# Weaving the first scores of three attentions, and the index scores of the third, into the projections before them

## The chip, the cores and the metric

One core of a Trainium2 chip runs the whole program in one launch. The metric is device time in microseconds (us). Engines are named as in the profile: PE is TensorE, PEld its weight loads, DVE is VectorE, ACT is ScalarE, SP issues the weight DMAs.

## What is computed

The reference is a stack of four layers on one sequence of 256 tokens and 1024 features, all in float32. The part that matters here is the three attentions with 16 heads of 64 features, each after a projection that makes queries, keys and values:

```python
# 1 (chunked): k, v from one product, q from another; a bias per head
sc = einsum('bqhd,bkhd->bhqk', qb, kb) + bias;  p = softmax(sc);  o = p @ v;  o @ w_o
# 2 (even): 8 "forgetting" heads with a cumulated gate, 8 window heads with a sink and rotations
o = concatenate([o_fox, o_swa], -1) @ w_out
# 3 (odd): index scores choose the 64 keys that each query sees
logits = einsum('bqhd,bsd->bqhs', iqi, ik)
score = einsum('bqh,bqhs->bqs', iwi, relu(logits));  _, idx = top_k(score, 64)
s = q . k[idx];  o = softmax(s) @ v[idx];  o @ w_out
```

Feed-forward layers follow each attention, the last one a mixture of eight experts.

## The kernel before

**Weights as a stream.** Every product takes its weights from one stream of slots of 1 MB (128 x 2048 floats). SP loads slots into six buffers `raw` (L358). For each slot ACT copies it, rounded, to `whi` (`split`, L1055), and DVE makes the remainder `wlo = raw - whi` (L1527); both have three buffers (SPL). PE then multiplies a slot in `product` with three passes each (L437, L438, L439): 24 products 512 wide in all, first 12 for the first 128 tokens, then 12 for the second 128. A projection 512 wide takes two slots. `mid(j)` is called between the two halves of slot j, `after(j)` behind it. The stream order, `Plan`, also has modulation slots (`ada`): DVE reduces one with the conditioning vector (`modulate`, L1548 and L1550, four passes); after every second, PE turns the sum into a column (`ada_turn`, L646) and DVE takes it (`ada_cols`, L1572).

**Order by hand.** There is no planner: each engine's program is an in-order list, and semaphores join them. On ACT and DVE `used` counts the slots consumed and `split(n)` prepares slots up to n; `take` and `take_scaled` on ACT empty a finished product from PSUM (L1109, L1121) and raise `acc_free`.

**Before an attention.** Queries and keys are turned on PE in rounds of up to four 128 x 128 transposes (`rounds`, L529) into PSUM banks 6 and 7, and ACT copies each out (`copies`, L1092). In the first attention the last two rounds of keys' source and all four of the queries stand behind the last slot or near it; in the second, eight rounds of `fq` and `fk` stand around and behind the last slot.

**An attention** (`attention` in each engine) goes over eight pairs of heads. For pair p: PE `scores(p)` (L680); DVE `mask(p)`, adding a mask and taking the minimum (L1856); ACT `exps`, one call for each head, with the sum (L1245), and for window heads also the sink's exponential (L1249); DVE `weigh(p)` (L1866, L1869); PE `turn(p)`, six transposes into banks 6 and 7 (L691); DVE and ACT each copy one half out (L1877, L1257); PE `values(p)` (L703). After each second pair ACT and DVE split the output into `xhi` and `xlo` (L1261, L1882). Then the output projection's product begins. DVE has the first two of its slots, and the modulation behind the second, ready before `mask(0)`.

**The third attention** first has its own work. Its projection has five parts (slots 2, 1, 2, 2, 2): index queries; index key and weights; queries in two parts; keys and values. DVE rotates them (`rope`, L1906 to L1911, six operations for each 128 tokens). After the fourth part PE makes 16 index products (L846), ACT a relu of each (L1379), DVE adds each to `score` (L2059, L2061). DVE then finds the 64 largest in eight rounds (L2078, L2080), and makes the mask `dsab` (L2086 to L2096). `mask(0)` needs it. Fourth and fifth part are on either side of the index products.

**After an attention** comes its residual: DVE adds both halves of the output to `h`, in the second and third attention with a gate (L1635, L1636); in the second, `residual_normed` goes on to squares, root, normalisation (L1698) and transposes (L546) before the next product can start.

Of the kernel before, what the change touches and what calls it, by code (L numbers as in the profile page):

```python
# [26 lines left out]
P = 128  # L27
# [71 lines left out]
class Plan:  # L99
# [3 lines left out]
    def __init__(self):  # L103
# [38 lines left out]
        proj("q", D, layer=0, behind=odd)  # L142
# [4 lines left out]
        proj("e_in", E_IN, E_ORDER, layer=1, behind=odd[1:])  # L147
# [43 lines left out]
def build_program(nc, x_in, cols_in, rows_in, vg_in, fg1_in, fg_in, pos_in, ws_in, toep_in, rw_in, stream_in, out):  # L191
# [3 lines left out]
    with ctx:  # L195
# [69 lines left out]
        SM_C, PT_C = (sm_0, sm_1, two_of(tok[:, 0:768])), (two_of(tok[:, 1024:1792]), two_of(tok[:, 2048:2816]))  # L265
        SM_E, PT_E = (sm_0, sm_1, two_of(tok[:, 0:768])), (two_of(tok[:, 5376:6144]), two_of(tok[:, E_W:E_W + 768]))
# [19 lines left out]
        rt_o = [af[:, 1280 + n * 288:1280 + (n + 1) * 288] for n in range(4)]  # L286
        score = af[:, 2432:2944].rearrange("p (t k) -> p t k", t=NT)
        left = af[:, 2944:3456].rearrange("p (t k) -> p t k", t=NT)
        relu = af[:, 3456:3968].rearrange("p (b k) -> p b k", b=2)
# [27 lines left out]
        def head(q, k, v, mask, h):  # L317
# [6 lines left out]
        EVEN = ([head(fqT[:, hh], fkT[:, hh], te[:, :, E_FV + hh * DH:E_FV + (hh + 1) * DH],  # L324
                      lambda t: causal[:, S - (t + 1) * P:S], hh) for hh in range(8)]
                + [head(half(sqT, hh, hh // 2), half(skT, hh, hh // 4), te[:, :, E_SV + hh // 4 * DH:E_SV + (hh // 4 + 1) * DH],
                        lambda t: window[:, S - (t + 1) * P:S], 8 + hh) for hh in range(8)])
# [103 lines left out]
        def _(pe):  # L431
# [218 lines left out]
            def gate_blocks(layer, g, hf):  # L650

                def after(j):
                    if j == 1 or (layer == 1 and (g, hf) == (0, 1)):
# [10 lines left out]
            def attention(units, name, sm, pT, after=None, mid=None):  # L664
# [5 lines left out]
                cols_made = turned_before(name)  # L670
                if cols_made:
                    pe.wait_ge(sem("ada_taken"), cols_made)

                def scores(p):
                    if p >= 2:
                        pe.wait_ge(sem("att_m"), 2 * (b + p - 1))
                    for t in range(NT):
                        for e in range(2):
                            a = units[2 * p + e]
                            m = pe.matmul(ps[:, (4 if p % 2 else 2 * sc) + e, parts(t)], a["q"][:, t * P:(t + 1) * P],  # L680
                                          a["k"][:, 0:(t + 1) * P], start=True, stop=True)
                    m.then_inc(sem("att_s"), 1)
# [1704 lines left out]
```

## Time and profile before

| | us |
|---|---|
| three runs | 1570.97, 1572.42, 1575.75; median 1572.42 |
| the profiled execution | 1572.48 |
| its span in the trace | 1570.7 |
| DVE / ACT / PE busy | 1240.2 / 915.9 / 1471.8 |
| stretch from a projection's last product to the output projection's first: first, second, third attention | 34.49, 34.44, 44.68 |

The span is what the trace holds; 1.8 us lie around it. Engine times are sums of their instructions; matmuls are pipelined, and each is shown with its own end, so that they overlap a little.

### The profile page before, as it was taken

How to read it: one execution, taken by the hardware profiler on the slowest of the kernel's cores; microseconds unless marked ns; L12 is line 12 of the kernel's file. 1: busy time of each engine (PE TensorE's matmuls, PEld its weight loads, DVE VectorE, ACT ScalarE, POOL GpSimd, SP SyncE). 2: the span in 40 equal slices, each digit the busy share in tenths (PEclk: the TensorE clock that was granted, in tenths of full speed). 3: DMA queues.
4: the chain of work that ended last, by engine and by line, in shares of the span. 5: the costliest groups of instructions: out<-in, count | busy, mean ns of one | idle time of the engine just before them, and what ended most of it. 6: DMA issues, size and time to landing. Idle time of an engine off the chain costs nothing.

```text
span 1570.7 us, 19868 instructions
## 1 busy us (share of the span) xinstructions
PE 1471.8 (94%) x7238; PEld 1200.2 (76%) x7239; DVE 1240.2 (79%) x1722; ACT 915.9 (58%) x1202; POOL 5.1 (0%) x17
## 2 busy tenths in 40 slices
PE   7999999997999998988899998959999999999995
PEld 5888888885788887866788887747778878877883
DVE  6767889768667888777777886795888888898887
ACT  6656564547556654465433333554776787777674
POOL 0000000000000000000000000000000000000000
PEclk9999999999999999999999998979999999999997
DMA  9654448873345467643567784312588889888882
GB/s 350 235 222 154 173 168 302 318 270 134 134 164 192 167 227 269 241 161 111 186 254 267 252 320 172 108 54 81 200 323 306 312 302 338 307 312 325 303 315 92
DMA packets 53416, 358.16 MB, mean 228 GB/s; under 512 B 6096, under 2 KB 7120, under 8 KB 12640
## 3 DMA queue, kind: packets, MB, share of 16 engines
q1 hardware_dynamic: 52736, 354.77, 60.9%
q0 software_dynamic: 176, 2.13, 0.4%
q8 instruction: 45, 0.74, 0.2%
q10 hardware_dynamic: 432, 0.30, 0.1%
q14 instruction: 27, 0.22, 0.0%
HBM read 356.13 MB, written 1.05 MB: 227 GB/s over the span
## 4 chain that ended last, share of the span: by engine, by line
PE 68%; DVE 17%; ACT 7%; issue 6%; DMA 1%; PEldq 0%; DVEq 0%; PEld 0%; ACTq 0%; SPq 0%
PE ps L437 21%; PE ps L439 20%; PE ps L438 20%; DVE wlo L1527 6%; ACT whi L1055 3%; PE ps L916 2%; PE ps L595 1%; DVE tok L2224 1%; PE ps L646 1%; PE ps L529 1%; DVE attn_scratch L1856 1%; DMA raw<-stream_dram 1%; DVE tok L1775 1%; ACT attn_scratch L1245 1%; DVE tok L1709 1%
## 5 line engine op out<-in xcount | busy, mean ns | idle before, releaser
L1527 DVE TENSOR_TENSOR wlo<-raw,whi 128x2048 fp32r<-128x2048 f32 (+2 forms) x304 | 651.3, 2165 | 144.1 <-ACT whi L1055 131.0
L1055 ACT ACTIVATE whi<-raw 128x2048 fp32r<-128x2048 f32 (+2 forms) x304 | 547.5, 1819 | 233.2 <-PE ps L439 228.3
L437 PE MATMUL ps<-whi,xhi 128*128 128x512 f32 (+3 forms) x1360 | 536.5, 394 | 19.5 <-DVE wlo L1527 9.4
L439 PE MATMUL ps<-whi,xlo 128*128 128x512 f32 (+3 forms) x1360 | 524.0, 385 | 0.0
L438 PE MATMUL ps<-wlo,xhi 128*128 128x512 f32 (+3 forms) x1360 | 523.8, 385 | 0.0
L437 PEld LDWEIGHTS ps<-whi,xhi 128*128 128x128 f32 x1360 | 258.2, 190 | 81.0 <-DVE wlo L1527 13.0
L439 PEld LDWEIGHTS ps<-whi,xlo 128*128 128x128 f32 x1360 | 257.9, 190 | 52.3
L438 PEld LDWEIGHTS ps<-wlo,xhi 128*128 128x128 f32 x1360 | 258.5, 190 | 47.0
L437 PE MATMUL ps<-whi,ahi 128*128 128x512 f32 x440 | 177.9, 404 | 5.2 <-DVE wlo L1527 5.1
L439 PE MATMUL ps<-whi,alo 128*128 128x512 f32 x440 | 174.1, 396 | 0.0
L438 PE MATMUL ps<-wlo,ahi 128*128 128x512 f32 x440 | 173.2, 394 | 0.0
L1550 DVE SCALAR_TENSOR_TENSOR acc<-raw,cs,acc 128x512 f32<-128x512 f32 x168 | 126.2, 751 | 5.1
L437 PEld LDWEIGHTS ps<-whi,ahi 128*128 128x128 f32 x440 | 82.6, 188 | 28.8 <-DVE wlo L1527 8.9
L1775 DVE SCALAR_TENSOR_TENSOR tok<-ps,cols,tok 128x255 f32<-128x255 f32 (+1 forms) x176 | 72.7, 476 | 37.0 <-ACT tok L1205 36.2
L439 PEld LDWEIGHTS ps<-whi,alo 128*128 128x128 f32 x440 | 82.6, 188 | 20.3
L438 PEld LDWEIGHTS ps<-wlo,ahi 128*128 128x128 f32 x440 | 82.7, 188 | 18.4
L1109 ACT ACTIVATE tok<-ps,st 128x512 f32<-128x512 f32 x64 | 40.6, 686 | 45.8 <-PE ps L595 30.7
L1210 ACT ACTIVATE tok<-tok 128x512 f32<-128x512 f32 x22 | 14.0, 634 | 65.6 <-DVE tok L1775 65.6
L1205 ACT ACTIVATE tok<-ps,cols 128x256 f32<-128x256 f32 x88 | 42.7, 576 | 3.8 <-DVEq L1793 3.8
L1245 ACT ACTIVATE attn_scratch<-attn_scratch,sx 128x128 f32<-128x128 f32 x72 | 32.0, 445 | 19.8 <-DVE sx L1856 19.8
L680 PE MATMUL ps<-head_scratch 64*128 64x128 f32 (+3 forms) x192 | 29.1, 419 | 11.8 <-DVE sx L1856 9.5
L1439 ACT ACTIVATE tok<-ps 128x256 f32<-128x256 f32 (+1 forms) x48 | 17.7, 368 | 35.1 <-PE ps L439 35.0
(286 smaller groups left out, 1179.9 us busy)
## 6 DMA issues: line engine op xcount, KB each, us to landing
raw<-stream_dram SPq DMA_DIRECT2D x317, 1024.0 KB, 5.1
raw<-stream_dram SPq DMA_DIRECT2D x32, 512.0 KB, 4.3
attn_scratch<-toep_dram POOLq DMA_DIRECT2D x1, 2048.0 KB, 9.5
raw<-stream_dram SPq DMA_DIRECT2D x2, 528.0 KB, 4.4
h<-x_dram SPq DMA_DIRECT2D x2, 512.0 KB, 4.8
y<-tok SPq DMA_DIRECT2D x2, 512.0 KB, 2.7
head_scratch<-w_s_dram SPq DMA_DIRECT2D x1, 512.0 KB, 14.2
head_scratch<-vg_dram SPq DMA_DIRECT2D x1, 512.0 KB, 11.2
```

Source lines behind the costliest of these rows:

```text
L437: pe.matmul(o, xh, wh, start=start, stop=False)
L438: pe.matmul(o, xh, wl, start=False, stop=False)
L439: return pe.matmul(o, xl, wh, start=False, stop=stop)
L680: m = pe.matmul(ps[:, (4 if p % 2 else 2 * sc) + e, parts(t)], a["q"][:, t * P:(t + 1) * P], a["k"][:, 0:(t + 1) * P], start=True, stop=True)
L916: m = pe.matmul(ps[:, 5 + 2 * b, k * P:(k + 1) * P], TA[:, t, (4 * b + k) * P:(4 * b + k + 1) * P], G[:, t, :], start=t == 0, stop=t == NT ...
L1055: act.activation(whi[:, q % SPL, 0:w], raw[:, s % RAW, 0:w], ACT.Copy).then_inc(sem("hi_done"), 1)
L1109: m = act.activation(dst[:, t], src[:, t], func, scale=st[:, 6 + t:7 + t])
L1205: m = act.activation(conv[:, f, :], ps[:, 6 + f // 2, (f % 2) * S:(f % 2 + 1) * S], ACT.Identity, scale=sc, bias=bi)
L1245: m = act.activation(x, x, ACT.Exp, bias=neg_max(u, t), scale=-1.0, accum_out=total(u, t))
L1527: dve.tensor_tensor(wlo[:, q % SPL, 0:w], raw[:, s % RAW, 0:w], whi[:, q % SPL, 0:w].bitcast(F32), ALU.subtract).then_inc(sem("lo_done"), 1)
L1550: m = dve.scalar_tensor_tensor(acc[:, :], wk, cs[:, kk:kk + 1], acc[:, :], ALU.mult, ALU.add)
L1775: m = dve.scalar_tensor_tensor(o, src, cols[:, c:c + 1], o, ALU.mult, ALU.add)
```

## The change

- **Pieces between slots.** `scores` of pairs 0 and 1 become a function `first_scores`, called between the two last slots of the projection (first and second attention), or before the attention (third). The transposes that they need are moved ahead of them; the last rounds (queries 2 and 3, or the fox keys) run inside the attention, just before `turn(0)` (`between`). On ACT `exps` of the first four heads come before the last part is taken.
- **Splits.** Only the first slot of the output projection is prepared ahead of the attention. DVE prepares the second at the attention's end, `hold` puts off the modulation behind it until the last `lo`.
- **Modulation slots** behind the last slot of the projection go one slot earlier (`Plan`).
- **Second attention:** window heads come first; the rows of its output weights are rolled to match. Third score buffers go to other places.
- **Third attention:** four batches of four index products stand in the halves and between slots of parts three and four; four relu buffers in place of two; rotations for both halves of tokens at once, four operations in place of twelve; selection rounds around the last slots; the mask's last two steps made in one.

```diff
-        proj("q", D, layer=0, behind=odd)
+        proj("q", D, layer=0, behind=(1, 2))
-        proj("e_in", E_IN, E_ORDER, layer=1, behind=odd[1:])
+        proj("e_in", E_IN, E_ORDER, layer=1, behind=(3, 5, 7, 8))
...
+            def first_scores(units, name):
+                pe.wait_ge(sem("acc_free"), T("acc"))
+                scores(units, 0)
+                cols_made = turned_before(name)
+                if cols_made:
+                    pe.wait_ge(sem("ada_taken"), cols_made)
+                scores(units, 1)
...
-                scores(0)
-                for i in range(n + 2):
+                for i in range(1, n + 2):
                     if i + 1 < n:
-                        scores(i + 1)
+                        scores(units, i + 1)
+                    if i == 2:
+                        between()
...
+            def first_queries(j):
+                if j == 0:
+                    pe.wait_ge(sem("acc_free"), T("acc"))
+                    two(TA, 0)
+                    two(TA, 1)
+            def first_chunked(j):
+                if j == 0:
+                    pe.wait_ge(sem("tr_free"), T("tr", 1))
+                    first_scores(CHUNKED, "attn_out")
+                    pe.wait_ge(sem("tr_free"), T("tr"))
+            proj(W, mid=first_queries, after=first_chunked)
...
+            proj(width[2], mid=lambda j: index_scores(0) if j == 1 else None, after=index_turns)
+            proj(width[3], mid=lambda j: None if j else index_scores(2), after=gate_turns)
+            proj(width[4], after=gate_blocks(1, 1, 1, 0))
...
+            keys(3)
+            split(used[0] + 3)
+            queries(0)
+            queries(1)
+            for u in range(4):
+                exps(CHUNKED, u)
+            take_scaled(TA[:, :, W:D], ahead=1)
+            queries(2)
+            queries(3)
             attention(CHUNKED, PT_C)
...
+            split(used[0] + 3)
             copies([skT], first=2)
-            split(used[0] + AHEAD + 1)
             copies([fqT[:, 2 * r:2 * r + 2, :] for r in range(4)], scale=DH ** -0.5, first=3)
-            take(te[:, :, E_FV:E_FG])
+            for u in range(4):
+                exps(EVEN, u)
+            take(te[:, :, E_FV:E_FG], ahead=1)
...
+                split(used[0] + 2, hold=True)
+                lo(3)
                 split(used[0] + SPL)
-                lo(3)
...
+            def rotate(first, heads):
+                dve.tensor_tensor(xc, x, table(cosT), ALU.mult)
+                link(dve.tensor_tensor(xs, x, table(sinT), ALU.mult))
+                dve.tensor_tensor(part(x, 0), part(xc, 0), part(xs, 1), ALU.subtract)
+                link(dve.tensor_tensor(part(x, 1), part(xc, 1), part(xs, 0), ALU.add))
...
+            split(used[0] + 3)
+            add_index(0)
+            split(used[0] + 4)
+            add_index(1)
+            used[0] += 2
+            next_pair()
+            add_index(2)
+            split(used[0] + 3)
+            add_index(3)
+            both(lambda t, nk: dve.tensor_tensor(score[:, t, 0:nk], score[:, t, 0:nk], causal[:, S - nk:S], ALU.add))
+            link(dve.tensor_scalar(causal[:, :], causal[:, :], NEG, None, ALU.add))
+            used[0] += 2
+            next_pair()
+            split(used[0] + 2)
+            dve.wait_ge(sem("acc_free"), T.up("acc"))
+            rotate(0, 8)
+            largest(0)
+            dve.wait_ge(sem("acc_free"), T.up("acc"))
+            rotate(W, 8)
+            dve.sem_inc(sem("rope_done"), 1)
+            for n in range(1, 5):
+                largest(n)
+            used[0] += 2
+            next_pair()
+            split(used[0] + 1)
+            dve.wait_ge(sem("acc_free"), T.up("acc"))
+            rotate(2 * W, 4)
+            dve.sem_inc(sem("rope_done"), 1)
+            for n in range(5, TOPK // 8):
+                largest(n)
...
-            both(lambda t, nk: dve.tensor_scalar(gt[:, t, 0:nk], gt[:, t, 0:nk], -NEG, NEG, ALU.mult, ALU.add))
-            both(lambda t, nk: dve.tensor_tensor(dsab[:, t, 0:nk], gt[:, t, 0:nk], causal[:, S - nk:S], ALU.min))
+            both(lambda t, nk: dve.scalar_tensor_tensor(dsab[:, t, 0:nk], gt[:, t, 0:nk], -NEG, causal[:, S - nk:S],
+                                                        ALU.mult, ALU.add))
```

## Rows read from the trace of the kernel before

**Rows 1.** The page: the chain that ended last, shares of the span by engine

```profile
PE 68%; DVE 17%; ACT 7%; issue 6%; DMA 1%; PEldq 0%; DVEq 0%; PEld 0%; ACTq 0%; SPq 0%
```

**Rows 2.** Windows (us, busy of PE, PEld, DVE, ACT, POOL, clock, DMA share, GB/s)

```profile
362.65:397.14 34.49, 25.03 (x197) 17.42 (x196) 28.71 (x105) 26.76 (x85) 0.00 (x0) 0.90 0.25 98
687.65:722.09 34.44, 26.73 (x192) 18.89 (x191) 28.17 (x108) 27.28 (x98) 0.00 (x0) 0.90 0.15 59
1022.48:1067.16 44.68, 26.69 (x192) 18.57 (x190) 42.11 (x156) 26.59 (x86) 0.00 (x0) 0.77 0.13 47
1002.98:1011.29 8.31, 6.88 (x36) 5.25 (x34) 5.02 (x13) 5.94 (x16) 0.00 (x0) 0.79 0.34 127
```

**Rows 3.** Timeline of PE, first attention (start us, us, engine, line, operation)

```profile
356.92 0.48 PE L437 MATMUL ps<-whi,xhi 128*128 128x512 f32 x1
...
375.91 0.94 PE L691 MATMUL ps<-ident,attn_scratch 128*128 128x128 f32 x6
```

**Rows 4.** Timeline of DVE, first attention

```profile
371.79 0.29 DVE L1856 CUSTOM_DVE_ANT_0 attn_scratch<-ps,attn_scratch 128x128 f32<-128x128 f32 x1 [0.27 <-PE ps L680]
...
379.58 1.03 DVE L1869 TENSOR_TENSOR tok<-tok,sx 128x256 f32<-128x256 f32 x2
```

**Rows 5.** Timeline of ACT, first attention

```profile
364.46 1.91 ACT L1055 ACTIVATE whi<-raw 128x2048 fp32r<-128x2048 f32 x1
366.26 1.26 ACT L1109 ACTIVATE tok<-ps,st 128x512 f32<-128x512 f32 x2
368.82 1.09 ACT L1092 ACTIVATE head_scratch<-ps 128x512 f32<-128x512 f32 x2 [0.32 <-PE ps L529]
```

**Rows 6.** Timeline of PE, second attention

```profile
679.50 1.61 PE L529 MATMUL ps<-ident,tok 128*66 128x128 f32 x8 [1.65 <-ACT head_scratch L1092]
...
680.76 0.78 PE L437 MATMUL ps<-whi,xhi 128*128 128x512 f32 x1
```

**Rows 7.** Timelines of ACT and DVE, second attention

```profile
703.90 0.47 ACT L1249 ACTIVATE sx<-rows,sx 128x1 f32<-128x1 f32 x2
705.15 0.47 ACT L1249 ACTIVATE sx<-rows,sx 128x1 f32<-128x1 f32 x2
...
700.80 1.03 DVE L1869 TENSOR_TENSOR tok<-tok,sx 128x256 f32<-128x256 f32 x2
```

**Rows 8.** Timeline of ACT, gate of the even layer: a table load and what follows

```profile
651.31 1.28 ACT L1344 ACT_TABLE_LOAD   x1
652.61 0.22 ACT L1344 ACTIVATE attn_scratch<-attn_scratch 128x16 f32<-128x16 f32 x1
```

**Rows 9.** Groups of DVE, window 722.09 to 744.28, and PE's timeline behind it

```profile
L1527 DVE TENSOR_TENSOR wlo<-raw,whi 128x2048 fp32r<-128x2048 f32 x4 | 9.2, 2294 | 5.8 <-ACT whi L1055 5.6
L1550 DVE SCALAR_TENSOR_TENSOR acc<-raw,cs,acc 128x512 f32<-128x512 f32 x4 | 3.0, 751 | 0.1
...
747.80 1.64 PE L546 MATMUL ps<-ident,tok 128*128 128x128 f32 x8 [1.79 <-DVE tok L1698]
```

**Rows 10.** Groups by line of DVE, window 982 to 1041.8, third attention

```profile
L1527 DVE TENSOR_TENSOR wlo<-raw,whi 128x2048 fp32r<-128x2048 f32 x6 | 13.6, 2290 | 4.3 <-ACT whi L1055 4.3
L2061 DVE SCALAR_TENSOR_TENSOR attn_scratch<-attn_scratch,st 128x128 f32<-128x128 f32 (+1 forms) x14 | 5.9, 418 | 0.7
L2078 DVE MAX8 mx<-attn_scratch 128x8 f32<-128x128 f32 (+1 forms) x16 | 5.0, 352 | 0.4
L2080 DVE MATCH_REPLACE8 attn_scratch<-mx,attn_scratch 128x128 f32<-128x128 f32 (+1 forms) x14 | 4.7, 343 | 0.0
```

**Rows 11.** Timelines of PE (first line) and DVE, third attention

```profile
989.80 1.04 PE L529 MATMUL ps<-ident,tok 128*128 128x128 f32 x8
976.92 0.46 DVE L1906 TENSOR_TENSOR attn_scratch<-tok,cosT 128x288 f32<-128x288 f32 x1 [0.41 <-ACT tok L1121]
...
1036.39 0.54 DVE L2086 TENSOR_SCALAR attn_scratch<-attn_scratch,mx 128x128 f32<-128x128 f32 x2
1041.81 0.29 DVE L1856 CUSTOM_DVE_ANT_0 attn_scratch<-ps,attn_scratch 128x128 f32<-128x128 f32 x1
```

More of the change, by code:

```diff
@@ L662, in gate_blocks, with scores, attention @@
                 return after
-            def attention(units, name, sm, pT, after=None, mid=None):
+            def scores(units, p):
+                b, sc = T.n.get("att", 0), chunk_n[0] % 2
+                if p >= 2:
+                    pe.wait_ge(sem("att_m"), 2 * (b + p - 1))
+                for t in range(NT):
+                    for e in range(2):
+                        a = units[2 * p + e]
+                        m = pe.matmul(ps[:, (4 if p % 2 else 2 * sc) + e, parts(t)], a["q"][:, t * P:(t + 1) * P],
+                                      a["k"][:, 0:(t + 1) * P], start=True, stop=True)
+                m.then_inc(sem("att_s"), 1)
+            def first_scores(units, name):
[5 more added lines that the diff above has]
+                scores(units, 1)
+            def attention(units, name, sm, pT, after=None, mid=None, between=lambda: None):
                 n = len(units) // 2
@@ L1098, in next_pair, with chunk @@
                 return pair((chunk_n[0] - 1) % 2, w)
-            def chunk(slots=2):
+            def chunk(slots=2, ahead=AHEAD):
                 used[0] += slots
-                split(used[0] + AHEAD)
+                split(used[0] + ahead)
                 act.wait_ge(sem("w_used"), used[0])
@@ L1110, in by_tile, with take_scaled, take @@
                 return m
-            def take_scaled(dst, func=ACT.Copy, slots=2):
-                chunk(slots)
+            def take_scaled(dst, func=ACT.Copy, slots=2, ahead=AHEAD):
+                chunk(slots, ahead)
                 by_tile(dst, next_pair(), func).then_inc(sem("acc_free"), 1)
-            def take(dst, func=ACT.Copy, w=W, scale=1.0, heads=None):
-                chunk(len(slots_of(KT, w)))
+            def take(dst, func=ACT.Copy, w=W, scale=1.0, heads=None, ahead=AHEAD):
+                chunk(len(slots_of(KT, w)), ahead)
                 src = next_pair(w)
@@ L1234, in gated_ffn, with exps @@
                 T.up("tr", n)
+            def exps(units, u):
+                b = T.n.get("att", 0)
+                act.wait_ge(sem("att_m"), 2 * b + u + 1)
+                for t in range(NT):
+                    x = units[u]["sm"][:, parts(t)]
+                    m = act.activation(x, x, ACT.Exp, bias=neg_max(u, t), scale=-1.0, accum_out=total(u, t))
+                if units is EVEN and u < 8:
+                    c = R_SK + u
+                    for t in range(NT):
+                        m = act.activation(sink(u, t), rows[:, c:c + 1], ACT.Exp, bias=neg_max(u, t))
+                m.then_inc(sem("att_e"), 1)
             def attention(units, pT):
@@ L1381, in _ @@
+            index_relus(3)
+            take(part_of[3])
+            take_gate(1, 0)
+            split(used[0] + 3)
+            take_gate(1, 1)
+            take(part_of[4], ahead=1)
             copies([qT[:, 2 * r:2 * r + 2, :] for r in range(4)], scale=DH ** -0.5)
@@ L2069, in both, with largest @@
                 dve.wait_ge(sem("dve"), T.up("dve", NT))
[L2071 to L2076 removed]
+            def largest(n):
                 src = score if n == 0 else left
```

255 lines of the change are left out of this document (124 added, 131 removed).

## The prediction

> **What bounds the kernel now.** I read the chain that ended last first: PE holds 68% of it, DVE 17%, ACT 7% [rows 1]. So over the whole span the products set the time, and a change that adds no products can only win where PE isn't at them. Second come windows cut to the three stretches between a projection's last product and the output projection's first. They last 34.49, 34.44 and 44.68 us, 113.6 in all, and DVE is busy in 28.71, 28.17 and 42.11 of them, more than PE or ACT in each [rows 2]. In an attention the pairs follow DVE; in the third, the selection of keys stands ahead of it as well. The reader is to see that there PE waits, and that what counts is how early DVE gets through its list, counted from the end of the projection. Third, I took each stretch apart in the timelines of the three engines.
>
> **The first attention.** Now the last product ends at 362.65 [rows 2]; then come a modulation turn and transposes, and `turn(0)` starts at 375.91 [rows 3]. ACT splits a slot (1.91 from 364.46) before it empties the product (1.26), and the last two copies start only at 368.82 [rows 5]. DVE has its first mask at 371.79, and `weigh(2)` ends at 379.58 + 1.03 = 380.6 [rows 4]. From there to the output product at 397.14 [rows 2] are 16.5 us of DVE at its own pace, and I let that stand.
>
> With the change, two rounds of transposes more, the fourth of the keys, the turn and two sets of scores lie before the last slot: about 0.45 x 3, 0.8 and 1.6 us at full clock, so the last product ends near 366.4. None of it is extra work. While this last slot runs (5.73 us, 356.92 to 362.65 now [rows 2, 3]) DVE does masks 0 and 1 (about 2.3) and `weigh(0)` (1.2), and ACT four exponentials. After 366.6: scores 2 and 3 1.6 us; ACT empties in 1.26 beside them, to 368; two rounds of transposes with a copy each (1.09 the pair [rows 5]) end at 370.0; `turn(0)` at 370.2. ACT's exponentials 4 and 5 wait for the two copies and end at 371.9, so `weigh(2)` ends at 373.6. That is 380.6 - 373.6 = **7.0 us** earlier. Bounds: if the last queries cost what the four rounds do now, 2.5 less, 4.5; if DVE never waits, its 21.7 us of remaining list start at 366.4, so 9.1. I stay between, since the copies' wait is read from this stretch.
>
> **The second attention.** The same, with window heads first. Now a 1.65 us wait of PE for ACT stands in the fox queries, and the last slot takes 6.89 us (680.76 to 687.65), at a partly lower clock [rows 2, 6]. The change moves the slot's split ahead of the copies, which removes that wait; I put the last slot at 5.5, from 682.5 to 688.0. ACT's window exponentials come 1.25 us apart (703.90 to 705.15 [rows 7]), so four take 5.0 and end at 687.6, just in time to empty the last part by 689.1. Four rounds of fox keys with ACT's copies follow to 692.8, then exponentials 4 and 5 to 695.4. From here, `weigh(2)` ends at 696.6 against 701.8 now (700.80 + 1.03 [rows 7]). Behind it one window pair is left in place of four, whose pace is ACT's (3.4 us a pair against DVE's 2.72): from 696.6 to the product 17.1 us, that is 713.7 against 722.09, **8.4 us**. Bounds: 4.5 as above, and 10.
>
> ACT loads the Exp table here between the fox queries' copies and the first exponential. In the trace a load takes 1.28 us and the next ACTIVATE starts 1.30 after it began [rows 8]; I count that, and it ends as the first mask does. The Trainium skill (ScalarE: Activation LUTs, "What ACT_TABLE_LOAD costs") puts a drain of some 1.38 us behind each load. By that page exponentials and everything behind them would be 1.4 us later and my total 1.4 us higher; the trace's row shows no such drain.
>
> **What is pushed behind.** In both, one `lo` (2.29) and one modulation (four passes, 3.0 in all [rows 9]) leave DVE's list ahead of the attention and land after it, 5.3 us together. Behind the first attention, DVE's waits swallow them before its next adding to `h`: I take nothing, with up to 0.5 against it. Behind the second, DVE waits 5.6 us for ACT's splits before 744.28 [rows 9]; 1.5 of it, ahead of the first `lo`, stays, so some 4.0 can be filled. The gated adding that comes then is on PE's path, which stands idle 1.79 until 747.80 [rows 9]. I charge 5.3 - 4.0 = **1.3 us** back. Net for the second: 7.1.
>
> **The third attention.** Index matmuls in a hole of 8.31 us [rows 2] now, DVE's selection behind them. Until the transposes at 989.80 [rows 11] the kernel is as before; in the changed one they come after the first slot of part three, one slot (5.45) earlier, at 984.4. Two us of turning and half a slot (2.7) put the first index products at 989.1, relus at 989.3. The four batches then go by halves of slots, with ACT's split of slot 7 between the third and fourth; DVE gets that slot's `lo` done at 1001.6, and waits no more. Its list from there, at prices of now:
> - four index additions of 256, 0.53 each, 2.1 (14 of both sizes are 5.9 us busy [rows 10]); causal mask and its shift 0.85;
> - two `lo`, 2.24 from start to start, 4.5 (13.6 busy for six in the stretch now [rows 10]);
> - rotations of 8, 8 and 4 heads: the elements are the same, with 12 operations in place of 36; one of 288 elements now takes 0.46 [rows 11], 0.38 start to start, of which 0.07 to 0.1 is fixed, so 3.55, 3.55 and 2.05 in place of 4.23, 4.49 and 2.88: 9.15;
> - eight selection rounds, 10.7 (5.0 and 4.7 and loads [rows 10]);
> - final steps, now 1036.39 to 1041.81 [rows 11], 5.42, less 0.46 for the step merged: 4.96.
>
> Sum 32.2: `mask(0)` starts at 1033.8 against 1041.81, **8.0 us** earlier. Scores of pairs 0 and 1 are there in both. From mask to product 25.35 us in the first attention and in the third alike (371.79 to 397.14, 1041.81 to 1067.16 [rows 2, 4, 11]), so I keep that. Bounds: 5, if each batch costs DVE another wait of 0.75; 11, if half of DVE's present waits in this stretch vanish.
>
> **Sum.** 7.0 + 7.1 + 8.0 = 22.1 us from 1572.48, the profiled execution's own time (span 1570.7 and 1.8 around it): **1550.4**. The median of the runs, 1572.42, is the same number. Everything outside these stretches and the two products behind them I cost at nothing: no product, transpose, or DMA is added, only their order changes. SP's queue has the same slots, two fewer fetched ahead at each attention's end; DMA is at a share of 0.25 or less in these stretches [rows 2], which covers it.
>
> **Rivals.**
> - The pushed work is paid in full (15%). Both 5.3 us packets delay the residuals behind, in place of the 1.3 I charge: 9.3 back, 1559.7. For it speaks that DVE is nearly full there; against it that its waits are seen.
> - The third gains nothing (10%): the four index batches make DVE and PE wait for each other as the hole does now, 8.0 back, 1558.4. For it: 16 relus and additions stay a strict chain. Against: half a slot is 2.7 us and a batch needs about 1.8.
> - The clock (9%): the short work between slots lets it fall to 1.2 GHz, as around 680, where a slot took 6.89 in place of 5.73 [rows 2, 3, 6]. Four such places in the first two, 1.16 each: 4.6 back, 1555.0. In the third PE has time to spare.
> - No change (3%): the first two rivals together, 22.1 - 9.3 - 8.0 = 4.8, about 1567.7.
> - Slower (3%): the index batches in the slots block. Every batch would stop PE for its products, four relus, a split on ACT, a `lo` and four additions, 1.0 + 1.8 + 1.9 + 2.3 + 2.1 = 9.1, four times 36.4, in place of the hole of 8.31. Part five would end at 1022.5 - 8.3 + 36.4 = 1050.6, and taking it, rotation, three rounds and final steps (1.0 + 2.05 + 3.5 + 4.96) at 1062.1, 20.3 late; less 14.1 from the others that is 1578.7. It decides from 7.6 us a batch, where the gain of the others is just used up. Against it: the splits for the next slot are placed ahead of or between the batches.
>
> **How the numbers follow.** The forecast has 60%, the rest stands above. A change of 0.3%, 4.7 us, is about the least that a measurement of this kernel can tell from none. Lower bounds of the gains, 4.5 + 3.2 + 5, give 12.7, hence 1559.8; the first rivals reach 1559.7. Upper bounds, 9.1 + 8.7 + 11, give 28.8 and 1543.7. So 1543 to 1561. Faster 0.94, same 0.03, slower 0.03.
>
> **What would show it.** First masks (L1856) start while three-pass products still run. The three stretches from last to first product shrink to about 24, 26 and 42 us (the projections' ends move later by 3.7 and 0.4, in the third earlier by 5.5), and the index hole is gone. Behind the second attention PE's wait for the normalised tokens grows to about 3.2 us. Wrong would be: products before an attention with new gaps over a microsecond, DVE waiting over 2 us inside the selection, or granted clock at 0.5 in the last slots.

## The result, and the profile after

| | us |
|---|---|
| after, four runs | 1551.29, 1551.51, 1552.13, 1558.15; median 1551.82 |
| before, four runs beside them | median 1572.37 |
| ratio after / before | 0.9875, 95% interval 0.9859 to 0.9892 |
| the profiled execution of after | 1551.29, its span 1549.5 |

So 20.5 us faster by the medians, 21.2 between the two profiled executions; 1550.4 had been predicted. Page of after, busy shares and the chain that ended last, to be held against [rows 1]:

```profile
PE 1463.6 (94%) x7238; PEld 1194.7 (77%) x7239; DVE 1236.5 (80%) x1689; ACT 913.1 (59%) x1202; POOL 5.1 (0%) x17
...
PE 68%; DVE 18%; ACT 6%; issue 6%; DMA 1%; PEldq 0%; DVEq 0%; PEld 0%; ACTq 0%; SPq 0%
```

The shares have hardly moved, and no engine's work fell by more than 1%: the gain is waiting that is gone. (PE's 8.2 us less are the same 7238 instructions at a mean granted clock of 0.979 in place of 0.973; more on this under the clock, below.) Windows from a projection's last product to the output's first, of after (same columns as [rows 2]):

```profile
367.71:391.23 23.52, 18.25 (x161) 12.51 (x161) 20.41 (x80) 18.39 (x64) 0.00 (x0) 1.00 0.00 1
681.08:706.25 25.17, 21.19 (x168) 15.80 (x169) 21.33 (x83) 20.50 (x73) 0.00 (x0) 1.00 0.00 1
1002.67:1044.35 41.68, 26.32 (x194) 18.27 (x191) 39.24 (x147) 26.50 (x86) 0.00 (x0) 0.80 0.07 26
```

They were 34.49, 34.44 and 44.68, and "about 24, 26 and 42" were predicted. They alone don't say what was gained, since the projections ahead of them grew. For that I use a ledger: the start of the first product of chosen weight slots in both traces, and by how much it comes earlier. A difference that changes from one line to the next was won or lost between them.

```
slot  what it is                         before    after   earlier by
 53   first projection, late slot        339.15   339.72    -0.57
 54   the next one                       345.08   347.18    -2.10
 56   its last slot                      356.92   361.98    -5.06
 57   first output projection            397.14   391.23     5.91
103   second projection, last slot       680.76   675.34     5.42
104   second output projection           722.09   706.25    15.84
108   next layer, first slot             751.33   736.21    15.12
109   next layer, second slot            760.47   746.15    14.32
142   third projection, first part       965.10   951.19    13.91
149   its last part                     1011.29   991.05    20.24
151   third output projection           1067.16  1044.35    22.81
155   first expert                      1108.72  1087.98    20.74
      end of the span                   1570.7   1549.5     21.2
```

At slot 52 the changed kernel is 0.4 ahead already. Slot 95, a fixed point ahead of the second attention, is 6.07 earlier. So the first attention gained 5.5 (0.4 to 5.91), the second 9.8 (6.07 to 15.84), and the third 8.9 (13.91 to 22.81). Four losses stand between: 0.7, 0.8 and 0.4 behind the second, 2.1 in the router.

**First masks under products.** PE (two lines) and DVE of after, first attention; the product of the last slot starts at 361.98:

```profile
361.66 0.38 PE L671 MATMUL ps<-head_scratch 64*128 64x256 f32 x2
361.98 0.50 PE L437 MATMUL ps<-whi,xhi 128*128 128x512 f32 x1
```
```profile
361.44 0.29 DVE L1932 CUSTOM_DVE_ANT_0 attn_scratch<-ps,attn_scratch 128x128 f32<-128x128 f32 x1 [0.63 <-PE ps L671]
...
368.61 0.29 DVE L1932 CUSTOM_DVE_ANT_0 head_scratch<-ps,attn_scratch 128x128 f32<-128x128 f32 x1 [3.35 <-PE ps L671]
...
373.69 1.03 DVE L1945 TENSOR_TENSOR head_scratch<-head_scratch,sx 128x256 f32<-128x256 f32 x2
```

The first mask was at 371.79 [rows 4] and is at 361.44, half a microsecond before the last slot. Masks 0 and 1 and `weigh(0)` are done under the product; then DVE idles 3.35 until the scores of pair 2. `weigh(2)` ends at 374.72, 5.9 earlier. From there to the output product are 16.5 us, as before: the gain is made ahead of this point.

**The index hole is gone.** PE of after, all four batches; the 8.31 us of [rows 2] have become four stops of 0.71 to 1.14:

```profile
972.87 0.71 PE L869 MATMUL ps<-head_scratch 64*128 64x128 f32 x8
976.46 0.71 PE L869 MATMUL ps<-head_scratch 64*128 64x128 f32 x8
980.05 1.14 PE L869 MATMUL ps<-head_scratch 64*128 64x256 f32 x8
984.06 1.13 PE L869 MATMUL ps<-head_scratch 64*128 64x256 f32 x8
```

DVE of after, the same stretch. It waits 3.96, 2.38 and 0.72 for relus and a split, and then only twice for 0.15 until the mask:

```profile
973.70 0.29 DVE L2147 TENSOR_SCALAR attn_scratch<-attn_scratch,st 128x128 f32<-128x128 f32 x1 [3.96 <-ACT attn_scratch L1423]
...
981.27 0.35 DVE L2147 TENSOR_SCALAR attn_scratch<-attn_scratch,st 128x256 f32<-128x256 f32 x1 [2.38 <-ACT attn_scratch L1423]
...
983.90 2.29 DVE L1600 TENSOR_TENSOR wlo<-raw,whi 128x2048 fp32r<-128x2048 f32 x1 [0.72 <-ACT whi L1095]
986.11 2.04 DVE L2149 SCALAR_TENSOR_TENSOR attn_scratch<-attn_scratch,st 128x256 f32<-128x256 f32 x4
...
1019.03 0.29 DVE L1932 CUSTOM_DVE_ANT_0 attn_scratch<-ps,attn_scratch 128x128 f32<-128x128 f32 x1
```

**A stall that nobody had predicted** stands ahead of slot 54. The chain that ended last, of after, in order of time (start, us, what):

```profile
332.33 0.45 PE ps L529 x4
...
333.30 1.92 ACT whi L1095
...
339.66 2.20 DVE wlo L1600
341.93 0.40 DVE acc L1624
342.36 0.76 DVE acc L1626
...
344.91 0.44 DVE xhi L1689
...
346.43 0.70 DVE xlo L1690
347.18 0.50 PE ps L437
```

A transpose at 332.33 releases ACT's `keys(0)`, a split stands behind that, and through DVE's remainder, modulation and tail the chain reaches PE, which waits 1.29:

```profile
347.18 0.50 PE L437 MATMUL ps<-whi,xhi 128*128 128x512 f32 x1 [1.29 <-DVE xlo L1690]
```

Before, that split started at 328.79: the copies of keys were not yet in front of it.

### The profile page after: what moved, and what is told of

It reads as the page before. It is cut to its first block, busy times and chain, and to the rows that moved or that the text cites. A ratio compares the mean times of both kernels' runs of the same rounds, so it can differ in the third digit from the quotient of the medians.

```text
span 1549.5 us, 19836 instructions
## 1 busy us (share of the span) xinstructions
PE 1463.6 (94%) x7238; PEld 1194.7 (77%) x7239; DVE 1236.5 (80%) x1689; ACT 913.1 (59%) x1202; POOL 5.1 (0%) x17
## 4 chain that ended last, share of the span: by engine, by line
PE 68%; DVE 18%; ACT 6%; issue 6%; DMA 1%; PEldq 0%; DVEq 0%; PEld 0%; ACTq 0%; SPq 0%
PE ps L437 20%; PE ps L439 19%; PE ps L438 19%; DVE wlo L1600 6%; ACT whi L1095 3%; PE ps L956 2%; PE ps L595 1%; DVE tok L2337 1%; PE ps L529 1%; PE ps L646 1%; DVE tok L1851 1%; DMA raw<-stream_dram 1%; DVE acc L1626 1%; DVE attn_scratch L1932 1%; DVE xlo L1690 1%
## 5 line engine op out<-in xcount | busy, mean ns | idle before, releaser
L1281 ACT ACTIVATE attn_scratch<-attn_scratch,sx 128x128 f32<-128x128 f32 x80 | 35.4, 443 | 13.1 <-DVE sx L1932 13.0
L956 PE MATMUL ps<-tok 128*128 128x128 f32 x288 | 33.6, 275 | 0.0
```

What stands on the lines that cost most here:

```text
L956: m = pe.matmul(ps[:, 5 + 2 * b, k * P:(k + 1) * P], TA[:, t, (4 * b + k) * P:(4 * b + k + 1) * P], G[:, t, :], start=t == 0, stop=t == NT ...
L1281: m = act.activation(x, x, ACT.Exp, bias=neg_max(u, t), scale=-1.0, accum_out=total(u, t))
```

## Experiments

In each, "earlier by" and "costs" are differences of slots as in the ledger, each from one profiled execution; the diffs are cut, and against the changed kernel if nothing else is said; medians are of three or five rounds, with `before` run on the same chip (medians 1571.65, 1572.71, 1571.74, 1572.81 at the four times).

**The first two attentions alone.** The third's projection, rotations and selection are as before:

```diff
-            proj(width[2], mid=lambda j: index_scores(0) if j == 1 else None, after=index_turns)
...
+            for u in range(16):
```

> The first two attentions as changed, the third's projection, rotations and selection as before. Theory (the three parts add up, each by its own stretch): the trace of the changed kernel reaches the third's projection 13.9 us earlier and gains 8.9 in the third, so here 1572.4 - 13.9 = 1558.5 us, within 2 for where the clock falls. Rival (the third's gain needs what the first two leave behind, or the other way round): more than 3 us off that.

Measured 1564.5 (1560.84 to 1564.85), ratio 0.9943 (0.9924 to 0.9963), 6 us above what I expected. By the total alone the rival's condition, more than 3 us off, is met. By the ledger the gains are there: 5.3 at slot 57, and slots 103 to 104 take 30.90 as in the changed kernel (30.91; before 41.33), 14.1 in all at slot 104. Then it falls to 12.9 at slot 108, to 9.5 at slot 151 and to 7.5 at slot 155. A cost of pushed work explains the first step. The largest others are in places where this kernel is as before: slots 142 to 145 take 14.15 at a granted clock of 0.82 (before 11.70 at 1.00), slots 154 to 155 take 23.46 at 0.85 (before 21.41 at 1.00). They led to the experiments on the clock below.

**The third alone.** The first two as before, everything of the third as changed (the diff is against before).

```diff
+            proj(width[2], mid=lambda j: index_scores(0) if j == 1 else None, after=index_turns)
...
+                if units is ODD:
+                    split(used[0] + 2)
```

> Only the third attention's part of the change: index scores between slots, large rotations, selection around the slots, one slot fewer prepared ahead. Theory (parts add up): 1572.4 - 8.9 = 1563.5 us, mask(0) 67.8 us after the third projection's second product, where it is 76.7 before. Rival (they need each other): more than 3 us off.

Measured 1566.21 (1564.69 to 1567.72), ratio 0.9961 (0.9947 to 0.9976). From slot 142 to slot 151 it gains 7.3, where the profile of after gains 8.9. The first mask is at 1035.88, and with the 1.3 that this run is late at slot 142 that is 7.3 earlier than before: 69.5 behind slot 142, where I expected 67.8. The total is 2.7 above what I expected. The rival "the third gains nothing" falls here. The two parts' totals gain 7.1 and 5.4, 12.6 together, where the changed kernel gains 20.5 by its first four runs and 18.1 by the four of the repeat below; so it is the slots, not the totals, that show that the parts add up.

**Splits ahead, as before.** Both first slots of the output projections, and the modulation, are prepared ahead of the first two attentions again:

```diff
+            split(used[0] + 4)
             for u in range(4):
                 exps(CHUNKED, u)
-            take_scaled(TA[:, :, W:D], ahead=1)
+            take_scaled(TA[:, :, W:D], ahead=2)
...
-            skip(1)
-            used[0] += 2
-            next_pair()
-            split(used[0] + 1)
+            skip(2)
```

> The changed kernel, but in the first two attentions the output projection's second slot and the modulation behind it are again prepared before mask(0). Theory A (the prediction's count of DVE's list, every microsecond ahead of the masks is paid): 5.3 us each, less 0.7 that the second residual gets back, about 1561.7 us. Theory B (DVE stands idle 3.3 us ahead of mask 2 in the changed kernel, so part is covered; what is paid is ACT's late exponentials and take, 3.7 us each): about 1558.5 us. Theory C (the waits cover it all): 1551 to 1552 us.

Measured 1561.57 (1561.07 to 1564.42), ratio 0.9931 (0.9915 to 0.9948). The total is that of theory A, but not its parts: the first attention gains 4.5 less than in the changed kernel, the second 2.8 in place of 9.8, where 5.3 each had been counted. Rows of PE and DVE of this kernel, first attention, show the price:

```profile
364.32 0.93 PE L671 MATMUL ps<-head_scratch 64*128 64x128 f32 x8 [2.82 <-DVE shf L1650]
```
```profile
361.90 2.29 DVE L1602 TENSOR_TENSOR wlo<-raw,whi 128x2048 fp32r<-128x2048 f32 x1 [2.93 <-ACT whi L1095]
```

PE's scores of pair 1 wait 2.82 for a column that DVE takes only behind a remainder, which waits 2.93 for its split. In the second attention the same two waits are 4.02 and 4.96. Of the 15.3 us that the first two attentions gain, 4.0 are left. So weaving the scores in pays mainly where the other work is moved out of the way. It is one part of the change, not a trimming. The other half, the work moved away without the scores woven in, was not run.

**The modulation not held.** Behind the second slot it is done at once, ahead of the last `lo`:

```diff
-                split(used[0] + 2, hold=True)
+                split(used[0] + 2)
```

> The changed kernel, but the modulation behind the output projection's second slot runs in its place, ahead of the last lo, instead of being held behind it. Theory: the last lo comes 3.0 us later, the second slot of both output products waits about 1.8 us for it, 1551.8 + 3.6 = 1555.4 us, with a gap in PE after the first slot. Rival (there is room ahead of the second slot): 1551.8 us, no gap.

Measured 1557.8 (1551.47, 1557.68, 1557.92, 1558.07), ratio 0.9895 (0.9869 to 0.9920). Each output projection's second slot waits for `lo(3)`, here in the first one:

```profile
399.23 0.50 PE L437 MATMUL ps<-whi,xhi 128*128 128x512 f32 x1 [0.76 <-DVE xlo L1958]
```

That costs 0.9 in each (slots 57 to 58: 7.57 against 6.68; slots 104 to 105: 7.58 against 6.66), half of the 1.8 expected. The total is 2.4 above my 1555.4 all the same, and one run is as fast as the changed kernel; the profiled run, the slowest, has slots 142 to 145 at 14.16 and a clock of 0.82, where the changed kernel's profile has 11.69 at 1.00. Behind the second attention it also leaves PE's wait for the normalised tokens at 1.78, as it was, so there holding back mostly moves the 0.9 from one place to another (slots 104 to 108 take 30.60, and 30.42 in a second profile of the changed kernel at the same clock); behind the first it is a net gain of about 0.6.

**ACT's split ahead of the first keys.** The order that the chain above pointed at:

```diff
+            split(used[0] + 3)
             keys(0)
             take_scaled(TC[:, :, W:D])
```

> In the first attention ScalarE's split of the next slot is put ahead of its copies of the first keys. Theory: the stall of 1.3 us in front of the product at 347.2 comes from that order (the copy waits for a transpose, and split, VectorE's remainder and its tail stand behind it), so it goes, and first attention's product comes 1.3 us earlier: total 1550.3. Rival: the wait is put off to the copies, which the next transposes wait for (0.5 to 1 us), and nothing changes.

Measured 1549.81 (1548.77 to 1555.29), ratio 0.9868 (0.9848 to 0.9888). ACT splits at 328.13, before the copy, and PE no longer waits between transposes and slot 54:

```profile
328.13 1.92 ACT L1095 ACTIVATE whi<-raw 128x2048 fp32r<-128x2048 f32 x1
332.89 0.60 ACT L1132 ACTIVATE head_scratch<-ps 128x512 f32<-128x512 f32 x1 [2.85 <-PE ps L529]
```
```profile
344.95 0.60 PE L529 MATMUL ps<-ident,tok 128*128 128x128 f32 x4
345.30 0.48 PE L437 MATMUL ps<-whi,xhi 128*128 128x512 f32 x1
```

Slots 53 to 54 take 5.92 in place of 7.46: 1.5 us. Slots 52 to 53 take 6.76 in place of 7.19, 0.4 more, so that 2.0 are won from slot 52 and kept to slot 57. With it the first attention gains 7.5. The chain of the stall is shown by this run; 1.3 had been expected.

**The changed kernel again, and the clock.**

> The changed kernel, unaltered, again. Two times have been seen of it, about 1551.5 and once 1558.2. My theory: its ledger of slots repeats within 0.3 us wherever the granted clock is the same, and a total that differs comes from where the stretches at half clock fall against the products: 1551.5 if they fall as in the first profile, up to 1558 if not. The rival is that the order of work itself differs from run to run; then the ledger would part at a wait and not at a low stretch.

Measured 1554.61 (1551.81, 1553.10, 1556.13, 1557.08), ratio 0.9892 (0.9876 to 0.9909). With the first four that makes eight runs from 1551.3 to 1558.2, median 1552.6; against the before run beside these four the change is worth 18.1 us. The profiled one is as long as the first, but its ledger parts from it. The steps above a microsecond are low stretches, and the longer of the two has the lower clock each time: slots 94 to 95 take 1.3 more (clock 0.70 against 0.82), 108 to 109 1.1 less (0.83 against 0.73), 145 to 146 1.35 more, and 154 to 155 2.1 less. Windows of one slot (145 to 146) in four kernels, in the order before, after, after again, the third alone:

```profile
976.80:983.92 7.12, 7.12 (x27) 5.78 (x25) 4.96 (x13) 2.71 (x5) 0.00 (x0) 0.76 0.41 147
```
```profile
962.88:969.94 7.06, 6.81 (x38) 5.54 (x35) 6.52 (x6) 3.85 (x7) 0.00 (x0) 1.00 0.43 149
```
```profile
963.83:972.24 8.41, 8.16 (x36) 6.56 (x35) 6.41 (x6) 3.75 (x6) 0.00 (x0) 0.83 0.43 142
```
```profile
978.44:986.79 8.35, 8.10 (x36) 6.48 (x35) 6.32 (x6) 3.75 (x6) 0.00 (x0) 0.84 0.42 138
```

The same kernel takes 7.06 at a mean clock of 1.00 and 8.41 at 0.83. Before had its clock at 0.76 there, with fewer transposes in the window. The gain of the third is 8.9 only where the changed kernel escapes this stretch; with it, as before has it, it is 7.3 (slots 142 to 151 take 102.06 before, 94.78 in the second profile, 94.77 in the third alone). In the profile of after, 1.6 of the third's gain was luck of the clock, and 2.1 in the router bad luck. Over the eight runs, those up to 1553.1 have a mean clock of 0.978 to 0.980 and those from 1556.1 on 0.975 or 0.976.

**The router filled.** A try to keep the clock up where TensorE idles between the halves of the router's transposes:

```diff
             for t in range(NT):
+                if t:
+                    keep_on(4)
```

> Four throwaway products of 512 columns are added on TensorE between the two halves of the router's transposes, where it idles while VectorE adds the second half of the residual. Theory: the 2.1 us that the changed kernel gives back between slots 151 and 155 are a stretch of half clock that begins in that idle time; filled, the clock stays up and the first expert comes 2.1 us earlier, total about 1549.7. Rival: the low stretch falls by its own count, at whatever work is there; then the four products only cost their own time, 0 to 0.9 us.

Measured 1554.38 (1551.13 to 1557.50), as the changed kernel. The profile is of the slowest of the four runs. Windows from slot 154 to 155, in the order before, after, the split ahead of the keys (which does not touch the router), the router filled:

```profile
1087.31:1108.72 21.41, 18.49 (x120) 15.80 (x120) 12.52 (x40) 11.14 (x22) 0.00 (x0) 1.00 0.09 36
```
```profile
1064.49:1087.98 23.49, 21.34 (x121) 18.23 (x120) 12.51 (x40) 11.12 (x22) 0.00 (x0) 0.85 0.16 59
```
```profile
1063.80:1085.20 21.40, 18.47 (x120) 15.80 (x120) 12.51 (x40) 11.11 (x21) 0.00 (x0) 1.00 0.11 38
```
```profile
1070.19:1093.88 23.69, 22.14 (x125) 18.79 (x124) 12.52 (x40) 11.12 (x22) 0.00 (x0) 0.86 0.17 63
```

Four more products are there and the clock is low all the same. A kernel with the router untouched has it at 1.00. So filling this idle time does not keep the clock up reliably; the rival's own count is not shown either, and what decides it isn't settled by these runs.

**Rotations tile by tile.**

```diff
...
+                for t in range(NT):
+                    rope(to[:, t, first:first + heads * DH].rearrange("p (h d) -> p h d", h=heads), heads, t, rt_o)
```

> The third attention's rotations (of the index part too) go tile by tile again, twelve operations in the place of four for each width, all else as changed. Theory: my prediction's 0.07 to 0.1 us fixed for each operation, with 8, 8 and 4 heads on the list that ends with the first mask, gives back 0.7 + 0.9 + 0.8 = 2.4 us: the first mask 2.1 to 2.4 later, total 1553.7 to 1554.2. Rival: the rotations lie in waits of VectorE for products, and it costs under 0.5.

Measured 1553.25 (1552.62 to 1559.90), ratio 0.9893 (0.9869 to 0.9916); the total can't tell it from the changed kernel. Windows of DVE's list from the remainder ahead of the first rotation to the first mask, rotations by tile and then as changed:

```profile
989.69:1021.96 32.27, 20.41 (x104) 16.23 (x102) 30.87 (x97) 10.63 (x14) 0.00 (x0) 0.78 0.22 82
```
```profile
989.17:1019.03 29.86, 20.43 (x104) 16.24 (x102) 28.67 (x72) 10.64 (x14) 0.00 (x0) 0.81 0.23 91
```

Twelve rotation operations in place of 36 (the windows count one more at their edge, a mask's), and 2.41 us, all of it on the way to the mask. That is the part of the third's gain that fewer rotation instructions bring. I put the rest, about 4.9 of 7.3, down to the selection's earlier start and to the mask's merged last step; no run separates these.

**The index remainder in DVE's wait.** ACT's split ahead of emptying part three, DVE's remainder ahead of the third batch:

```diff
+            split(used[0] + 5)
             take(part_of[2])
             index_relus(2)
-            split(used[0] + 3)
...
+            split(used[0] + 3)
             add_index(2)
-            split(used[0] + 3)
             add_index(3)
```

> In the third attention ScalarE splits the slot for part five ahead of emptying part three, and VectorE makes its remainder ahead of the third batch of index additions, in place of behind it. Theory: the changed kernel's list of selection is set back at its start by two waits, 2.38 for relus and 0.72 for a split that stood behind relus; the remainder (2.29) fills them. Then the fourth batch, bound by TensorE's half slot, is next: its additions end about 1.0 earlier (987.1 in place of 988.15), and so do the first mask and the output product. Rival: the transfer of the slot or its buffer comes free no earlier, and nothing moves, or the third batch's products wait for the relus and TensorE loses up to 0.5.

Measured 1551.85 (1549.51 to 1553.77), ratio 0.9872 (0.9851 to 0.9892). DVE of this kernel:

```profile
981.29 2.29 DVE L1600 TENSOR_TENSOR wlo<-raw,whi 128x2048 fp32r<-128x2048 f32 x1 [0.77 <-ACT whi L1095]
...
986.90 2.04 DVE L2149 SCALAR_TENSOR_TENSOR attn_scratch<-attn_scratch,st 128x256 f32<-128x256 f32 x4 [1.49 <-ACT attn_scratch L1423]
```

Slots 149 to 151 take 52.48 in place of 53.30: 0.8 of the 1.0 expected. The waits of 2.38 and 0.72 have become 0.77 for the split and 1.49 for the fourth batch, as the theory said: what is late next is TensorE's half slot.

**A remainder behind the normalisation.** The second next slot's is taken from in front of the gated addition:

```diff
-                split(used[0] + 2)
+                split(used[0] + (2 if gained else 1))
...
                 normed(1)
+                split(used[0] + 2)
```

> Behind the second attention and behind the layer after it, the remainder of the second next slot (2.29) is taken from in front of the gated addition of the first 128 tokens to VectorE's later wait of 3.4 us for transposes. Theory: the work that was pushed out of the attention costs only because it stands there; TensorE's wait for the normalised tokens, 2.67, falls to about 0.5, slot 108 comes 2.0 (1.6 to 2.4) earlier against slot 104, and 1.2 to 1.6 are won before slot 141: total 3 to 4 us less, 1548 to 1549. Rival: the addition isn't waiting for VectorE but for the product's first half, and under 0.5 us is won at each.

Measured 1554.35 (1554.01 to 1554.58), no better than the changed kernel. PE of after, then PE of this kernel:

```profile
732.85 1.06 PE L546 MATMUL ps<-ident,tok 128*128 128x128 f32 x8 [2.67 <-DVE tok L1774]
736.21 0.77 PE L437 MATMUL ps<-whi,xhi 128*128 128x512 f32 x1 [2.30 <-DVE xlo L1780]
```
```profile
732.98 1.06 PE L546 MATMUL ps<-ident,tok 128*128 128x128 f32 x8 [0.81 <-DVE tok L1774]
742.56 0.50 PE L437 MATMUL ps<-whi,xhi 128*128 128x512 f32 x1 [0.75 <-DVE wlo L1600]
```

Slots 104 to 108 take 28.09 against 29.96 (30.42 in the second profile of after), where 2.0 less was expected, and the wait fell to 0.81. But slots 108 to 109 take 10.94 against 9.94 and 8.82 in the two profiles of after: PE now waits 0.75 for that very remainder, and 0.84 more ahead of slot 109. The clock is not what sets that slot's length. The kernel with all three steps (next experiment) shows this. Slots 108 to 109 here, and then there, with PE's wait for the remainder:

```profile
736.35:747.29 10.94, 9.35 (x32) 6.78 (x32) 8.18 (x16) 3.10 (x8) 0.00 (x0) 0.76 0.27 97
```
```profile
732.92:743.88 10.96, 8.50 (x33) 6.17 (x33) 8.18 (x16) 3.10 (x8) 0.00 (x0) 0.84 0.27 97
739.13 0.50 PE L437 MATMUL ps<-whi,xhi 128*128 128x512 f32 x1 [1.64 <-DVE wlo L1601]
```

At a higher clock the slot is as long, and PE's wait is longer. From 104 to 109 it is 39.03 here, against 39.90 and 39.24. So the wait had been moved on by one slot, and of the 2 us won 0.9 were kept against the one profile, 0.2 against the other.

**Together.** First all three, then only the two that held.

```diff
+            split(used[0] + 3)
             keys(0)
...
+            split(used[0] + 5)
             take(part_of[2])
             index_relus(2)
-            split(used[0] + 3)
...
```

> The split ahead of the first keys, the index remainder and the remainder behind the normalisation together. Theory: they lie in different stretches and add: 1.5 + 1.0 + 3.5 = 6.0 us from the changed kernel's 1551.3 to 1557 (median of both looks about 1552.6), so 1545.3 to 1551, median 1546.6. Rival: a saving ahead of a wait for transfers or clock is given back, and under half of it is left: 1549.6 or more.

Measured 1552.29 (1552.04 to 1555.84). Slot 57 is 1.6 earlier than in after and slot 151 only 0.3: slot 145 to 146 takes 9.29 at a clock of 0.74, and slots 154 to 155 take 25.00 at 0.80. The total is on the rival's side (1549.6 or more). The split's gain and the index remainder's are in the ledger (slots 53 to 54 take 5.93, 149 to 151 52.49), the third was none, and low stretches took back what there was.

> Only the two changes of order that held when tried alone: ScalarE's split ahead of the first keys, and the index remainder ahead of the third batch. Theory: 1.5 us by slot 57 and 0.85 more by slot 151, 2.3 in all from the changed kernel, whose eight runs so far go from 1551.3 to 1558.2 with the place of the stretches at half clock: so runs from 1549.0 to 1556, median near 1550.5. Rival: the low stretches move with the work and give it back, as in the combined kernel: median 1552 or more, though the ledger of slots still shows both gains.

Measured 1548.38 (1547.14, 1547.26, 1548.38, 1554.12, 1554.72), ratio 0.9864 (0.9840 to 0.9887). Slots 53 to 54 take 5.93 and slots 149 to 151 52.50, so both gains, 1.5 and 0.8, are there. It is 2.1 below the 1550.5 expected and has the lowest median of all kernels here, but its interval overlaps that of the changed kernel; the ledger, not the total, is the evidence.

## Why the prediction was right, and where its steps were not

The total was 0.9 off the first profile (1550.4 against 1551.29), and 2.2 off the median of all eight runs, 1552.6. Its terms were less exact than that: the first attention fell short by 1.5, the second and third were over by 1.4 and 0.9, and low stretches outside gave and took. That they nearly cancel is luck. The mechanism, masks under the last slot and a shorter way from there to the output product, is what the runs show.

- **First attention, 7.0 predicted, 5.5 measured.** The step that failed is "none of it is extra work": the last product ended at 367.71 and not near 366.4. The order of ACT's list had changed too, and its split now stood behind a copy that waits for a transpose. With that order mended the gain is 7.5. The gap of 1.29 is one of the prediction's own signs of being wrong, "products before an attention with new gaps over a microsecond", and it came. Inside the stretch the steps held: `turn(0)` 3.3 behind the last product (predicted 3.8) and `weigh(2)` 7.0 behind it (predicted 7.2), though DVE's idle time there, 3.35, appears in none of them.
- **Second attention, 8.4 predicted, 9.8 measured.** Set back to before's time (6.07 at slot 95), the last slot starts at 681.4 (predicted 682.5), and the output product at 712.3 (713.7). Of the 1.4 more, 1.1 were already won ahead of the last slot. The wait of 1.65 in the fox queries [rows 6] is gone, as predicted, and that slot takes 5.74 at full clock.
- **The table load.** ACT of after:

```profile
674.55 1.28 ACT L1281 ACT_TABLE_LOAD   x1
675.84 0.40 ACT L1281 ACTIVATE attn_scratch<-attn_scratch,sx 128x128 f32<-128x128 f32 x1
```

  The exponential starts 1.29 after the load began, as in [rows 8]. The drain of some 1.38 us that the Trainium skill states (ScalarE: Activation LUTs, "What ACT_TABLE_LOAD costs") is not seen; here the trace decides.
- **Pushed behind, 1.3 predicted.** Behind the second: 0.7 in the first profile and 1.2 in the second profile (slots 104 to 108: 29.24, 29.96, 30.42); the second is the like comparison, at a clock of 0.94 against 0.95 before, while the first has 0.98. The further 0.8 from 108 to 109 in the first profile is a low stretch (9.94 at 0.73; 9.14 at 0.80 before; 8.82 at 0.83 in the second profile). PE's wait for the tokens is 2.67, where about 3.2 was written. Behind the first: 0.3 to 0.4 (slots 57 to 94: 227.29 before, 227.59 and 227.70), within the 0.5 allowed. The rival "paid in full" is out.
- **Third attention, 8.0 predicted, 8.9 measured,** but 7.3 where the clock is as in before. The list from the remainder's end (986.19) to the first mask (1019.03) is 32.8 against 32.2: rotations took 3.68, 3.69 and 2.08, 9.45 in all against 9.15, and DVE waited twice for 0.15 in a list that was to wait no more; the selection rounds (10.7), the remainders (2.21 from start to start against 2.24) and the final steps (4.95) agree. The list began 1.5 earlier than predicted, set back to before's time (1000.1 against 1001.6), and 1.35 of that is slot 145 to 146 at full clock. So the mechanism and the prices were right, and the excess over 8.0 is the clock's; with the clock as in before the forecast was 0.7 too high.
- **The clock.** I gave it 9% as a rival in the first two attentions, where it would have cost 4.6. The opposite came: both stretches are at 1.00, and were at 0.90 [rows 2]. Windows of before, from the last product's end to the first mask and from there to the end of `weigh(2)`, first attention:

```profile
362.65:371.79 9.14, 5.24 (x40) 4.40 (x41) 5.02 (x6) 6.90 (x9) 0.00 (x0) 0.86 0.54 209
371.79:380.61 8.82, 7.78 (x58) 5.16 (x56) 8.48 (x43) 7.56 (x32) 0.00 (x0) 0.76 0.43 164
```

  An estimate from these clocks (0.14 of 9.14 and 0.24 of 8.82 us are missing): at full clock PE's work there would have been at most 3.4 us shorter. How much of that was on the path, where DVE leads, no run separates, so the 5.5 and 9.8 hold an unknown part that the clock gave and that my sum doesn't name. It isn't chance: in all eleven profiles with these scores woven in and the splits moved, slots 56 to 57 and 103 to 104 are at 1.00; in the third alone they are at 0.92 and 0.84.
- **The step that failed** is "Everything outside these stretches and the two products behind them I cost at nothing": low stretches move over the program, and they took 2.1 in the router and gave 1.6 in the third. Runs of one kernel spread over 7 us, more than some terms of the sum, and the slower ones show the lower mean clock. It isn't the clock alone: the four runs with the index remainder moved go from 1549.51 to 1553.77 at one mean clock, 0.980.
- The slower rival (batches that block) needed 7.6 us a batch; the four stops are 0.71 to 1.14 long, and DVE is the one that waits.

## What to carry to other kernels

Where a serial stage follows a long product, put its first steps between the last slots, and move everything else that stands in those in-order queues out of the way; without the second half most of the gain is gone (splits ahead: 4.0 left of 15.3 us, and 9 us more in the total). For each step moved forward, list what is now queued behind it on that engine's queue too: one copy ahead of one split cost 1.5 us three hops later. Where a wait is taken away, look at the next slot before counting it: a remainder moved behind the normalisation won 1.9 in one slot and lost 1.0 or more in the next. Judge gains of a few microseconds by where fixed points of the work fall in both traces, not by the total.

## What was not expected of the hardware

- Stretches at half the clock (0.5 of full speed, so 1.2 GHz) fall in other places in other runs of one kernel. The same slot took 7.06 at a clock of 1.00 and 8.41 at 0.83; a stretch of the router 21.40 at 1.00 and 23.49 at 0.85. Work added there didn't prevent it in the one profile that has it. Why they fall where they do stays open. The level is seen where a window holds nothing else, in the router of after:

```profile
1076.49:1080.49 4.00, 4.00 (x15) 3.09 (x15) 3.38 (x14) 3.97 (x4) 0.00 (x0) 0.50 0.00 0
```

- An instruction's fixed share, estimated at 0.07 to 0.1 us, was confirmed by the count: 24 fewer rotation operations over the same elements saved 2.41 us, 0.10 each.
- A lower granted clock need not cost anything where another engine sets the pace: slots 108 to 109 took 10.94 at 0.76 and 10.96 at 0.84 in two kernels with the same order there.
